# Two converted halves of the input taken in another order, narrow projections by split stationary weights, and an MLP whose two products with one weight tile are merged

## The reference, cut to what matters

```python
# layer 0: input projection; q, k, v, z and gates come from one wide matrix
proj = x @ w_in                               # (256, 1024) @ (1024, 8208)
... beta_raw, a_raw = the last 8 + 8 columns  # one number per head and token
beta = jax.nn.sigmoid(beta_raw)
g = -jnp.exp(a_log) * jax.nn.softplus(a_raw + dt_bias)
# q, k, v: causal convolution of 4 taps over tokens, silu, then q and k are l2-normalized

# last layer: SwiGLU MLP, D_FF = 2816
gate, up = jnp.split(hn2 @ w_gate_up, 2, axis=-1)   # (256, 1024) @ (1024, 5632)
x = x + g2 * ((jax.nn.silu(gate) * up) @ w_down)    # (256, 2816) @ (2816, 1024)
```

## Time and profile before

| | |
|---|---|
| median of 3 runs | 1048.14 us (1047.56 to 1048.99) |
| span of the profiled execution | 1048.4 us |
| PE busy | 1019.6 us (97%) |
| PEld busy | 897.6 us (86%) |
| DVE busy | 752.1 us (72%) |
| ACT busy | 530.2 us (51%) |

### The profile page before, as it was taken

One profiled execution on the slowest core, in us unless ns is written; L12 is line 12 of the kernel. 1 busy time (PEld: TensorE's weight loads), 2 busy tenths in 40 slices (PEclk: granted clock), 3 DMA queues, 4 the chain that ended last, 5 costly groups with the idle time before them and its releaser, 6 DMA issues.

```text
span 1048.4 us, 21565 instructions
## 1 busy us (share of the span) xinstructions
PE 1019.6 (97%) x9120; PEld 897.6 (86%) x9120; DVE 752.1 (72%) x1049; ACT 530.2 (51%) x590; POOL 0.5 (0%) x7
## 2 busy tenths in 40 slices
PE   9999999999999999999999999989999999999998
PEld 7999999999866798989898787659986669999986
DVE  5999957678557668677787866867986775565553
ACT  5674544483353464435555433656687564335331
POOL 0000000000000000000000000000000000000000
PEclk8999999999999999999999999999999999999999
DMA  9454343244326664425343554876352446545441
GB/s 353 162 183 161 129 154 106 97 162 161 123 81 255 236 240 167 150 83 200 122 162 122 178 185 163 320 295 241 123 181 99 161 143 260 218 184 188 157 171 47
DMA packets 26302, 181.47 MB, mean 173 GB/s; under 512 B 3040, under 2 KB 3296, under 8 KB 4960
## 3 DMA queue, kind: packets, MB, share of 16 engines
q1 hardware_dynamic: 25056, 174.66, 45.2%
q10 hardware_dynamic: 1152, 5.45, 1.4%
HBM read 179.04 MB, written 1.05 MB: 172 GB/s over the span
## 4 chain that ended last, share of the span: by engine, by line
PE 87%; DVE 7%; ACT 3%; DMA 2%; issue 1%; SPq 0%; DVEq 0%; ACTq 0%
PE PS L916 84%; DVE WL L1799 2%; DMA RAW<-wst 1%; ACT WH L1386 1%; PE PS L1079 1%; DMA layer<-xt 1%; DVE X L1995 1%; DVE X L1996 1%; PE PS L1157 1%; PE PS L1307 0%; DVE STAT L1977 0%; DVE X L1976 0%; DVE layer_ln L2109 0%; DVE layer L2102 0%; ACT block L1690 0%
## 5 line engine op out<-in xcount | busy, mean ns | idle before, releaser
L916 PE MATMUL PS<-XTH,WH 128*128 128x256 f32 x1392 | 403.7, 290 | 6.2 <-issue 1.5
L916 PE MATMUL PS<-XTL,WH 128*128 128x256 f32 x1392 | 394.8, 284 | 0.0
L916 PE MATMUL PS<-XTH,WL 128*128 128x256 f32 x1392 | 394.7, 284 | 0.0
L1799 DVE TENSOR_TENSOR WL<-RAW,WH 128x2048 fp32r<-128x2048 f32 x138 | 314.2, 2277 | 99.8 <-ACT WH L1386 96.4
L1386 ACT ACTIVATE WH<-RAW 128x2048 fp32r<-128x2048 f32 x138 | 262.7, 1904 | 214.2 <-PE PS L916 208.7
L916 PEld LDWEIGHTS PS<-XTH,WH 128*128 128x128 f32 x1392 | 267.8, 192 | 12.6 <-issue 3.8
L916 PEld LDWEIGHTS PS<-XTL,WH 128*128 128x128 f32 x1392 | 268.0, 193 | 1.6 <-issue 1.4
L916 PEld LDWEIGHTS PS<-XTH,WL 128*128 128x128 f32 x1392 | 267.8, 192 | 0.0
L916 PE MATMUL PS<-WH,YH 128*128 128x512 f32 x224 | 89.6, 400 | 1.1 <-DVE YL L2274 1.1
L916 PE MATMUL PS<-WH,YL 128*128 128x512 f32 x224 | 87.4, 390 | 0.0
L916 PE MATMUL PS<-WL,YH 128*128 128x512 f32 x224 | 87.3, 390 | 0.0
(11 more groups left out here) (293 smaller groups left out, 1112.6 us busy)
## 6 DMA issues: line engine op xcount, KB each, us to landing
RAW<-wst SPq DMA_DIRECT2D x162, 1024.0 KB, 4.9
LNW<-lnrow ACTq DMA_DIRECT2D x3, 1024.0 KB, 6.7
RAW<-wst SPq DMA_DIRECT2D x4, 512.0 KB, 5.7
layer<-xt SPq DMA_DIRECT2D x2, 512.0 KB, 5.3
XR<-x ACTq DMA_DIRECT2D x1, 1024.0 KB, 4.7
out<-X SPq DMA_DIRECT2D x4, 256.0 KB, 3.3
CST<-cst ACTq DMA_DIRECT2D x1, 640.0 KB, 8.7
PT<-pt SPq DMA_DIRECT2D x1, 512.0 KB, 5.6
```

Source lines behind the costliest of these rows:

```text
L916: return pe.matmul(o, lhsT, rhs, start=start, stop=stop)
L1799: tt(WL[:, i % RAW_RING, 0:n], RAW[:, i % RAW_RING, 0:n], as_float(WH[:, k % SPLIT_RING, 0:n]), ALU.subtract).then_inc(vector_done, 1)
```

## The change

**The start.** `xs:0` comes first on both engines, before `split_top`, and `xs:1` directly after it. `ba` is rewritten: VectorE splits the 16 columns (step `wb`) into an fp32r tile `WBW`, 8 blocks of 16 high and 16 low columns; TensorE holds a 128-column window of it stationary and moves `XTH` and `XTL` past it, 16 matmuls of 256 columns, half of them ahead of `first:k:0:0` and half behind `k:0:0`. The result lies with features on partitions, so VectorE copies it out (`ba`), TensorE transposes it in a new step `bat` (2 matmuls) behind `k:0:1`, and VectorE (`bat`, 8 small instructions) adds high and low and spreads it. `ba1` moves behind the convolution `k:0:1` on both engines. One of the six matmuls of ones goes.

**The MLP.** `XTH` and `XTL` are now the two halves of one tile `XT`, at the addresses they had. Where a weight tile's high part was multiplied with `XTH` and with `XTL` in two matmuls of 256 columns, `features_wide` moves both past it in one of 512. A feature tile needs a bank of its own for this, with high x high and low x high in the left half and high x low in the right; a unit takes two banks, in the order (4, 5), (6, 7), (0, 1), (2, 3). ScalarE copies both right halves to SBUF (`ffc`), VectorE adds both left halves (`ffa`), ScalarE applies silu in place, VectorE multiplies and splits as before. The units run in plain order.

```diff
-    step("ba", on="TV", banks=(0,))
+    step("wb", on="V")
+    step("first", "ba", on="T", banks=(0,), readers="", half=0)
+    step("ba", on="TV", banks=(0,), opens=False, half=1)
+    step("bat", on="TV", banks=(1,))
...
+    wide = [(4, 5), (6, 7), (0, 1), (2, 3)]
     for j in range(FF):
-        unit("ff", j, on="TSV", slab=("ff", j), halves=False)
+        step("ff", j, on="TSV", banks=wide[j % 4], slab=(("ff", j),), readers="V", read_in=("ffa", j))
+        step("ffc", j, on="S")
+        step("ffa", j, on="V")
+    while ring[0] != 4:
+        bank()
...
 ORDER_S = """
-setup split_top xs:1 split:0:0 xs:0 split:1:1 ba1 split:2:2 split:3:3 k:0:0 split:4:4 k:0:1 split:5:5 ba2 norm:k:0
+setup xs:0 split_top xs:1 split:0:0 split:1:1 split:2:2 k:0:0 split:3:3 split:4:4 k:0:1 ba1 split:5:5 ba2 norm:k:0
...
+            def features_wide(step, ready):
+                split_ready(step.slabs[0])
+                wh, wl = wt(step, KC)
+                for k in range(KC):
+                    if k % 2 == 0:
+                        ready(k // 2)
+                    for a in range(2):
+                        s, o = slice(a * P, (a + 1) * P), PS[:, step.banks[a], :]
+                        mm(o.rearrange("p (x t) -> p x t", x=2), wh[:, k, s], XT[:, :, k, :], start=k == 0, stop=False)
+                        last = mm(o[:, 0:T], wl[:, k, s], XT[:, 0, k, :], start=False, stop=k == KC - 1)
+                return last
...
             def t_ba(step):
-                pe.wait_ge(x_loaded, 16)
-                pe.wait_ge(rest_loaded, 16)
-                pe.wait_ge(wba_loaded, 16)
-                for c in range(NT):
-                    for k in range(KC):
-                        last = mm(PS[:, 0, c * 16:(c + 1) * 16], XT0[:, k, c * P:(c + 1) * P], WBA[:, k, :],
-                                  start=k == 0, stop=k == KC - 1)
+                pe.wait_ge(vector_done, vector_at("wb"))
+                pe.wait_ge(vector_done, vector_at("xs", step.half))
+                for k in range(4 * step.half, 4 * step.half + 4):
+                    w = WBW[:, k * 32:k * 32 + P]
+                    mm(PS[:, 0, 0:T], w, XTH[:, k, :], start=k == 0, stop=False)
+                    last = mm(PS[:, 0, 0:T], w, XTL[:, k, :], start=False, stop=k == KC - 1)
                 last.then_inc(tensor_done, 1)
+
+            def t_bat(step):
+                pe.wait_ge(cst_loaded, 16)
+                pe.wait_ge(vector_done, vector_at("ba"))
                 for c in range(NT):
...
-            def s_ff(j):
+            def s_ffc(j):
                 act.wait_ge(tensor_done, tensor_at("ff", j))
                 if j >= 2:
                     act.wait_ge(vector_done, vector_at("ff", j - 2))
-                fn(SG[:, j % 2, :], PS[:, bank_of("ff", j), 0:T], ACT.Silu).then_inc(scalar_done, 1)
+                b = bank_of("ff", j)
+                fn(GU[:, j % 2 * 2:j % 2 * 2 + 2, :], PS[:, b:b + 2, T:2 * T], ACT.Copy).then_inc(scalar_done, 1)
...
+            def v_ffa(j):
+                dve.wait_ge(scalar_done, scalar_at("ffc", j))
+                b, both = bank_of("ff", j), GU[:, j % 2 * 2:j % 2 * 2 + 2, :]
+                tt(both, both, PS[:, b:b + 2, 0:T], ALU.add).then_inc(vector_done, 1)
```

More of the change, by code:

```diff
@@ L477 @@
 ORDER_T = """
-ba first:k:0:0 k:0:0 first:k:0:1 k:0:1 first:v:0:0 v:0:0 norm:k:0 first:v:0:1 first:q:0:0 v:0:1 gcc q:0:0 first:q:0:1
+first:ba first:k:0:0 k:0:0 ba first:k:0:1 k:0:1 bat first:v:0:0 v:0:0 norm:k:0 first:v:0:1 first:q:0:0 v:0:1 gcc q:0:0 first:q:0:1
 q:0:1 first:zb:0:0 zb:0:0 gc:0 first:zb:0:1 zb:0:1 first:k:1:0 k:1:0 norm:q:0 vtr:0 first:k:1:1 k:1:1 first:v:1:1
@@ L543 @@
 pv:15 rms:1:0:0 split:105:128 rms:1:0:1 split:106:130 rms:1:1:0 rma:1 rmt:1:0 rms:1:1:1 rmt:1:1 ada:10:1 xt:5:0 xt:5:1
[L544 to L549, removed]
+xt:5:2 xt:5:3 split:107:133 ada:11:1 ffc:0 split:108:134 ff:0 ffc:1 split:109:135 ff:1 ffc:2 split:110:136 ff:2 ffc:3
+split:111:137 ff:3 ffc:4 split:112:138 ff:4 ffc:5 split:113:139 ff:5 ffc:6 split:114:140 ff:6 ffc:7 split:115:141 ff:7
+ffc:8 split:116:142 ff:8 ffc:9 split:117:143 ff:9 ffc:10 split:118:144 ff:10 ffc:11 split:119:145 ff:11 ffc:12
+split:120:146 ff:12 ffc:13 split:121:147 ff:13 ffc:14 split:122:148 ff:14 ffc:15 split:123:149 ff:15 ffc:16
+split:124:150 ff:16 ffc:17 split:125:151 ff:17 ffc:18 split:126:152 ff:18 ffc:19 split:127:153 ff:19 ffc:20
+split:128:154 ff:20 ffc:21 split:129:155 ff:21 split:130:156 split:131:157 split:132:158 split:133:159 split:134:160
+split:135:161 split:136:162 split:137:163 split:138:164
 """
 ORDER_V = """
-split_top xs:1 split:0:0 xs:0 ba split:1:1 split:2:2 ba1 k:0:0 split:3:3 k:0:1 split:4:4 v:0:0 split:5:5 ba2 norm:k:0
+wb xs:0 split_top xs:1 split:0:0 split:1:1 ba split:2:2 k:0:0 split:3:3 bat k:0:1 split:4:4 ba1 v:0:0 split:5:5 ba2 norm:k:0
 gcc v:0:1 split:6:6 q:0:0 split:7:7 q:0:1 split:8:8 gc:0 split:9:9 split:10:10 k:1:0 split:11:11 vtr:0 norm:q:0
@@ L584 @@
 split:105:128 out2:0:1 out2:1:1 rmsb:1:0 rmsb:1:1 adat:10 xt:5:1 xtl:5:0 xt:5:3 xtl:5:1 xtl:5:2 xtl:5:3 split:106:130
[L585 to L590, removed]
+adat:11 split:107:133 ffa:0 split:108:134 ff:0 ffa:1 split:109:135 ff:1 ffa:2 split:110:136 ff:2 ffa:3 split:111:137
+ff:3 ffa:4 split:112:138 ff:4 ffa:5 split:113:139 ff:5 ffa:6 split:114:140 ff:6 ffa:7 split:115:141 ff:7 ffa:8
+split:116:142 ff:8 ffa:9 split:117:143 ff:9 ffa:10 split:118:144 ff:10 ffa:11 split:119:145 ff:11 ffa:12 split:120:146
+ff:12 ffa:13 split:121:147 ff:13 ffa:14 split:122:148 ff:14 ffa:15 split:123:149 ff:15 ffa:16 split:124:150 ff:16
+ffa:17 split:125:151 ff:17 ffa:18 split:126:152 ff:18 ffa:19 split:127:153 ff:19 ffa:20 split:128:154 ff:20 ffa:21
+split:129:155 ff:21 split:130:156 split:131:157 split:132:158 split:133:159 first:down:0:5 split:134:160 down:0:5
+split:135:161 split:136:162 split:137:163 split:138:164 first:down:1:5 down:1:5
 """
@@ L681, in build @@
         X = sb("X", [P, NT, D])
-        XTH = sb("XTH", [P, KC, T], F32R)
-        xtl_at = at[0]
-        XTL = sb("XTL", [P, KC, T], F32R)
+        xtl_at = at[0] + 4 * KC * T
+        XT = sb("XT", [P, 2, KC, T], F32R)
+        XTH, XTL = XT[:, 0], XT[:, 1]
         y_at = at[0]
@@ L755, in build @@
         AH, AC, AZ = A0.take(2 * T), A0.take(2 * T), A0.take(2 * T)
+        WBW = place("WBW", arena_at + 4 * A0.at, [P, KC * 32 + 96], F32R)
         ER = A0.take(4, P)
@@ L820, in build @@
         A3 = Arena("mlp", arena_at + 4 * 2048)
-        SG, HT = A3.take(2, T), A3.take(2, T)
+        GU = A3.take(4, T)
         eh_at = arena_at + 4 * 2048 + 4 * 4 * T
@@ L1347, in _ @@
             pe.wait_ge(gpsimd_done, gpsimd_at("setup"))
-            for _ in range(6):
+            for _ in range(5):
                 mm(PS[:, 7, :], ONES[:], ONES[:].unsqueeze(1).to_broadcast([P, 4, P]))
@@ L1408, in s_ba1 @@
             def s_ba1():
-                act.wait_ge(vector_done, vector_at("ba"))
+                act.wait_ge(vector_done, vector_at("bat"))
                 fn(flat(BE), TA, ACT.Exp, scale=-1.0)
@@ L2308, in _ @@
                      "feat": v_feat, "qn": v_qn, "mb": v_mb, "mlz": v_mlz, "xtl": v_xtl, "score": v_score, "ratio": v_ratio, "mln": v_mln,
-                     "out2": v_out2, "down": v_down, "ff": v_ff}
+                     "out2": v_out2, "down": v_down, "ffa": v_ffa, "ff": v_ff}
             dve.wait_ge(gpsimd_done, gpsimd_at("setup"))
```

51 lines of the change are left out of this document (37 added, 14 removed).

## The result

The changed kernel takes 1062.44 us (1061.43 to 1063.27, 4 runs) beside 1048.57 us for the kernel before (1047.56 to 1050.04, 4 runs): ratio 1.0122, 95% interval 1.0108 to 1.0136. It is slower, as predicted, but by 13.9 us and not by 8.1, and 1062.4 lies above the range. The profiled run of after has a time of 1062.62 us and a span of 1060.7. Measured again later (4 runs, median 1061.98 us beside 1049.79), the ratio was 1.0125 (1.0106 to 1.0143).

The account below looks back on a forecast made before the run. The prediction took TensorE, busy 97% of the span, as the bound. Start +4.8 and MLP +3.3 (4.5 + 1.0 + 2.0 - 4.2) gave +8.1 us on 1048.4, thus 1056.5, stated as 1056.3; range 1051.5 to 1059.5.

Parts of the forecast that it names:

- First unit early, clock up: At the start, TensorE begins its first unit at 10.0 us instead of 13.04, with its clock at 1.00 to 28 us.
- ScalarE's order holds `norm:k:0`: At the start, ScalarE splits slab 3 only after silu and square of `k:0:0`; `norm:k:0` begins at 35.7, +2.8 us.
- The clock after the gap, 2.0 us: TensorE's 7 us idle gap ahead of `norm:k:0` lets its clock fall to half, costing 2.0 us (1.5 to 2.5).
- The start in sum: Start of the kernel: 2.8 us for the late `norm:k:0` plus 2.0 for the clock, +4.8 us (bounds +2.8 and +6.3).
- `ff:0` and `ff:1` wait for banks 5 and 7: MLP entrance: banks still being read delay `ff:0` by 4.5 us and `ff:1` by 1.0; a clock fall adds 2.0.
- The rate: MLP products: one wide product replaces two narrow ones, saving 0.012 us for each of 352 pairs, -4.2 us.
- Sum: Whole kernel: start +4.8 and MLP +3.3 make +8.1 us on the profiled 1048.4; after the MLP all as before; 1056.3 us.
- The clock holds: Rival, chance 0.28: TensorE's clock stays up in one or both gaps, or later waits swallow part; 1053.9, down to 1051.
- The wide product saves nothing: Rival in the MLP, chance 0.08: the wide product with its operand in two pieces takes 0.24 us; 1060.5 us.
- The early start carries through: Rival at the start, chance 0.03: ScalarE and VectorE keep up, so TensorE keeps its 4.1 us lead without clock fall; 1047.3 us.

## Why the prediction was right or wrong

- **First unit early, clock up**: right (10.23 for a forecast of 10.0; 1.00 until 32.4).
- **ScalarE's order holds `norm:k:0`**: right. Forecast 35.7, measured 36.05; VectorE idle for 3.3, measured 3.44. Moving one name gave 3.4 us back.
- **The clock after the gap, 2.0 us**: right, 2.1 by the filled gap. The start in sum +4.8, measured +4.9, and 5.1, 5.3 and 6.2 in three further profiles of the same kernel; that the first agreed to 0.1 us is in part luck. One reading of the earlier trace rows was wrong without consequence: the clock of before fell at 11.9, during the narrow passes, and so ahead of the 1.14 us wait.
- **`ff:0` and `ff:1` wait for banks 5 and 7**: right; 4.5 forecast and 4.9 measured, then 1.0 + 2.0 forecast and 3.2 measured. The two lines that free the banks gave 8.3 us.
- **The rate**: the mechanism was right, the size was off, in both directions. In the usual pace the MLP gives back 4.5 to 4.9 us over 21 units (121.43 us before, 116.89 or 116.56 after) where the forecast had 4.0 for as many: a pair takes 0.3467 us for a forecast of 0.1201 + 0.2282 = 0.3483. In the first profile it gave only 2.6, by the slower pace. Nothing in the trace of before held that pace.
- **The step that failed is "Sum".** It closes with "after it all is as before", and for the stretch between the start and the MLP it has no term at all. The runs put one there: **+1.6 to +1.9 us** at 609 us, since with fewer instructions at the start the burst lies elsewhere in the blocks. It is in every profile of the changed kernel, also in the three with the usual pace, whose spans lie 9.5 to 10.9 us over the 1048.4 of before for the 8.1 forecast. By itself it doesn't explain the whole miss: without it, 1062.4 would be 1060.5, still above the range, which was built from known costs of up to +10.5 and had no room for a term left out. TensorE's issue waits stood on the page of before (1% of the chain), and I asked of each edit only what it does to rate, waits and clock.
- **The same step took a span for a time.** It set the profile's 1048.4 beside the median of 1048.14 and corrected by 0.2 us. In fourteen later runs of before the span lies 1.8 us under the time of the same run (1048.4 belongs to 1050.2). By this the profiled execution took about 1.6 us more than the median of 1048.57, and times of after lie 1.9 to 2.8 over their spans.
- Together, for the miss of 6.1: the middle 2.0, pace 1.6 (2.6 for 4.2), entrance 0.6, the profile's base about 1.6, which leaves 0.3. The spans of the two profiles differ by 12.3, the forecast by 8.1, and the first three make these 4.2. Which pace the three unprofiled runs of after had isn't known.
- **The rivals.** "The clock holds" had 0.28; both falls came. "The wide product saves nothing" has the nearest time, 1060.5, but by the wrong cause: a pair saved 13.3 ns (6.6 in the first profile's pace). The Trainium skill's gap from one matmul to the next ("TensorE: Matmul & The Clock Gate", "Wait — 56ns, not 53.3ns?": N / 2.4 + 2.5 ns), by which a pair would save 2.5 ns, doesn't hold for these pairs: 13.3 ns. The section that the prediction names, "Back-to-back issue gap", sets this formula apart as that of an isolated matmul. "The early start carries through" was out for this order only: with VectorE's and ScalarE's orders mended the work is 1.9 us ahead at 205 us, though the time shows no gain over the start of before.

## What to carry to other kernels

Where an in-order engine gets a new order, look at the two engines beside it: here TensorE got its first unit 2.8 us earlier and lost 4.9, since ScalarE stood behind silu with VectorE's next split, and with a better order of the same work it was 1.9 us ahead at 205 us, which the time didn't show. A product that takes a second bank takes that bank's last reader with it: compare what the readers of both do, and put the unit where they are done. And keep a reserve for what a changed number of instructions does behind bursts of small products: 1.6 to 1.9 us without any edit there.

## What the runs showed of the hardware

- 32 TensorE instructions more or fewer, 570 us earlier, decide whether TensorE is 1.6 to 1.9 us late behind a burst of small products. A packet of the instruction queue begins 0.2 to 0.5 us ahead of the burst's end where it is late, and 1.9 to 2.3 us behind it where it isn't.
- The same pairs of products run at 0.3467 or at 0.3534 us, each for a whole MLP, at one granted clock.
- A 256-column product among its like costs 13.3 ns beside its columns (120.0 - 106.7), a 512-column one with its operand in a single piece 14.9. A pair of a 512-column one with its operand in two pieces and a 256-column one costs 26.7 beside its columns (346.7 - 320.0).
- Filling a 7 us gap with 7 products of ones, of which nobody reads the result, is worth 2.1 us; the fall that it avoids lasted 6.8 us, and one of 10.2 us cost 0.9 to 1.4 us more.
